# Two weight pairs of the input projection ahead of the first norm's product on TensorE

## The reference

```python
xn = rms_norm(h, g_mix[l])                 # x * rsqrt(mean(x^2) + eps) * g
proj = xn @ w_in[l]                        # 1024 -> 2564 columns
pa, pb, pc, pd = jnp.split(proj, ...)      # short conv, dilated attention, forgetting attention + 4 gates, pool
...
logf = jax.nn.log_sigmoid(p[..., 3 * G:] + b_f)      # the 4 gate columns
...
h = act(feat @ w1 + b1)                    # second block: hyena filter network, act(a) = sin(freq * a)
h = act(h @ w2 + b2)
h = act(h @ w3 + b3)
```

## Time and profile before

| | |
|---|---|
| Median of 3 runs | 1575.12 us (1574.12 to 1576.87) |
| Span of the profiled execution, first to last instruction | 1572.3 us |
| Median of the runs less that span | 2.8 us |
| TensorE busy | 1495.1 us, 95% |
| VectorE busy | 952.0 us, 61% |
| ScalarE busy | 572.7 us, 36% |
| GpSimd busy | 125.7 us, 8% |
| Mean granted TensorE clock | 0.972 of full speed |

### The profile page before, as it was taken

How to read it: one execution, slowest core, us unless ns; L and a number is a source line. 1 busy time by engine, 2 the same in 40 slices (tenths; PEclk the granted TensorE clock), 3 DMA queues, 4 the chain that set the end, 5 groups by cost and what they waited for, 6 DMA issues and landing times.

```text
span 1572.3 us, 17974 instructions
## 1 busy us (share of the span) xinstructions
PE 1495.1 (95%) x6732; PEld 1210.7 (77%) x6732; DVE 952.0 (61%) x1215; ACT 572.7 (36%) x740; POOL 125.7 (8%) x117
## 2 busy tenths in 40 slices
PE   6999999879998999999999999999899999999996
PEld 5678667657886888888888778887688888888884
DVE  6776665763554567547637787789766533443346
ACT  4321562441433354323314454543333321321222
POOL 1000131220000000000000110154100000000000
PEclk8899999889999999999999999999999999999998
DMA  5222115114320222223232232234232323222231
GB/s 208 89 75 90 65 54 188 41 54 187 107 81 28 81 80 107 82 106 107 81 108 87 100 108 107 80 126 139 83 107 86 112 97 107 80 107 99 89 107 53
DMA packets 23486, 153.08 MB, mean 97 GB/s; under 512 B 2811, under 2 KB 2955, under 8 KB 7040
## 3 DMA queue, kind: packets, MB, share of 16 engines
q1 hardware_dynamic: 18720, 134.23, 24.1%
q0 software_dynamic: 3984, 15.68, 2.9%
q10 hardware_dynamic: 720, 2.30, 0.4%
HBM read 145.90 MB, written 6.30 MB: 97 GB/s over the span
## 4 chain that ended last, share of the span: by engine, by line
PE 86%; DVE 8%; ACT 3%; issue 2%; DMA 1%; POOL 0%; SPq 0%; DVEq 0%; ACTq 0%; POOLq 0%
PE ps L1359 26%; PE ps L1361 26%; PE ps L1360 26%; DVE w_lo L724 1%; PE ps L1698 1%; DMA raw<-weights_dram 1%; DVE opA_lo L767 1%; PE ps L1539 1%; ACT w_hi L392 1%; PE ps L1590 1%; PE ps L1558 1%; PE ps L1460 1%; PE ps L1685 1%; PE ps L1548 1%; DVE gen L1027 1%
## 5 line engine op out<-in xcount | busy, mean ns | idle before, releaser
L1359 PE MATMUL ps<-opA_hi,w_hi 128*128 128x512 f32 x1184 | 470.4, 397 | 15.3 <-DVE opA_lo L775 11.7
L1361 PE MATMUL ps<-opA_hi,w_lo 128*128 128x512 f32 x1184 | 464.5, 392 | 0.0
L1360 PE MATMUL ps<-opA_lo,w_hi 128*128 128x512 f32 x1184 | 464.5, 392 | 0.0
L392 ACT CAST w_hi<-raw 128x2048 fp32r<-128x2048 f32 x119 | 227.2, 1909 | 386.9 <-PE ps L1361 382.7
L724 DVE TENSOR_TENSOR w_lo<-raw,w_hi 128x2048 fp32r<-128x2048 f32 x119 | 277.8, 2335 | 126.0 <-ACT w_hi L392 125.8
L1359 PEld LDWEIGHTS ps<-opA_hi,w_hi 128*128 128x128 f32 x1184 | 224.8, 190 | 68.3 <-DVE w_lo L724 12.7
L1360 PEld LDWEIGHTS ps<-opA_lo,w_hi 128*128 128x128 f32 x1184 | 224.9, 190 | 47.4 <-issue 1.4
L1361 PEld LDWEIGHTS ps<-opA_hi,w_lo 128*128 128x128 f32 x1184 | 224.4, 190 | 47.8
L1359 PE MATMUL ps<-opB_hi,w_hi 128*128 128x512 f32 x608 | 238.9, 393 | 7.3 <-DVE spec L1251 2.6
L1360 PE MATMUL ps<-opB_lo,w_hi 128*128 128x512 f32 x608 | 238.1, 392 | 0.0
L1361 PE MATMUL ps<-opB_hi,w_lo 128*128 128x512 f32 x608 | 237.9, 391 | 0.0
(11 more groups left out here) (276 smaller groups left out, 1585.0 us busy)
## 6 DMA issues: line engine op xcount, KB each, us to landing
raw<-weights_dram SPq DMA_DIRECT2D x126, 1024.0 KB, 4.8
g_dram<-gen POOLq DMA_DIRECT2D x8, 512.0 KB, 3.6
h<-x_t_dram SPq DMA_DIRECT2D x4, 512.0 KB, 11.1
h<-x_t_dram POOLq DMA_DIRECT2D x1, 2048.0 KB, 12.4
scores<-g_dram POOLq DMA_DIRECT2D x4, 512.0 KB, 3.6
g_spec<-g_dram POOLq DMA_DIRECT2D x4, 512.0 KB, 3.6
out_dram<-h ACTq DMA_DIRECT2D x4, 512.0 KB, 2.7
mem_raw<-mem_t_dram POOLq DMA_DIRECT2D x1, 1024.0 KB, 10.7
```

The source lines that it names most:

```text
L392: A.copy(w_hi[:, p, :], raw[:, p, :]).then_inc(hi_ready, 1)
L1359: W.matmul(out, w[0], x[0], start=start, stop=False)
L1360: W.matmul(out, w[0], x[1], start=False, stop=False)
L1361: return W.matmul(out, w[1], x[0], start=False, stop=stop)
```

## The change

TensorE's calls of `in_pair(1, 0)` and `in_pair(1, 1)` move from behind `mlp(0)` to directly behind `in_pair(0, 1)`, ahead of the norm's product. No instruction is added or taken away, no other engine's stream is touched, and no semaphore count is changed.

```diff
@@ -1447,8 +1447,10 @@
-            in_pair(0, 0)
-            in_pair(0, 1)
+            for j in range(2):
+                in_pair(0, j)
+            for j in range(2):
+                in_pair(1, j)
             pe.wait_ge(made_ones, 1)
             pe.wait_ge(summed, KT)
             W.matmul(misc(0), ones[:], acc[:], start=True, stop=True).then_inc(misc_done, 1)
@@ -1463,8 +1465,6 @@
             last.then_inc(misc_done, 1)
             pe.wait_ge(small_in, 112)
             mlp(0)
-            for j in range(2):
-                in_pair(1, j)
```

## The result

| | median (range, runs) | span of the profiled execution |
|---|---|---|
| before | 1574.62 us (1573.32 to 1576.87, 4 runs) | 1572.3 us |
| changed | 1580.28 us (1579.3 to 1583.72, 4 runs) | 1577.5 us |

The ratio is 1.0041 with a 95% interval of 1.0027 to 1.0055. The forecast was 1580.9 us within 1577.4 to 1583.9, slower. The change costs 5.7 us by the medians and 5.2 us by the spans.

The account below looks back on a forecast made before the run. TensorE, busy 95% of the span, was taken as the bound. Own time -4.7, stall at rotate(0, 4) +8.2, slower second rotation +0.2 and restart +2.0 gave +5.8 us (rounded): 1580.9 us, range 1577.4 to 1583.9.

Parts of the forecast that it names:

- Step 1: Behind chunk 1: chunks 2 and 3 run gapless at full clock to 35.94, saving TensorE 4.7 us of gap and restart.
- Step 2: At the norm's product: it starts at 35.94 instead of 27.67, delaying VectorE and ScalarE by 8.3 us.
- Step 3: From norm to mlp(0) reads: faster gates help little; VectorE and ScalarE stay 8.3 us late, second read ending at 62.95.
- Step 4: At rotate(0, 4): TensorE waits for VectorE's reads, some 8 us in two pieces, products at 58.7 and 62.95.
- Two terms of the sum: TensorE's own time, -4.7 us, and its standing still at rotate(0, 4), +8.2 us.
- Step 5: After the stall: second rotation at half clock, chunks 4 and 5 take 12.95 us, ending at 77.86, +5.8 us.
- The term of 2.0 us: Chunks 4 and 5: the cost of restarting at half clock, 12.95 us instead of 10.94.
- Step 6: Behind chunk 5: VectorE is ready at 76.1, ahead of 77.86, so TensorE sets the pace and nothing is given back.
- Moves rigidly from there: Everything behind chunk 5 (cast of pair 4, rope(2, 6), mlp(1), chunk 6) comes 5.8 us later.
- TensorE's own time decides: Rival: saved gap and restart count, VectorE's reads come in time; -4.7 us, 1570.4 us, chance 0.04.
- The clock stays full at rotate(0, 4): Rival: no half-clock restart after the stall; +2.7 us, 1577.8 us, chance 0.07.
- A second slow spell: Rival: another stretch of the head also starts at half clock; +7.8 us, 1582.9 us, chance 0.08.

Follow-up runs that it names:

- e12: Changed kernel with rotate(0, 4) behind chunks 4 and 5 and VectorE's two mlp(0) reads back to back: ratio 1.0018, chunk 6 2.0 us late.
- e8: The changed kernel run and profiled once more, unaltered, against the kernel before: ratio 1.0041, median 1584.11 against 1576.54 us.
- e11: Kernel before, with VectorE's rotary arguments put ahead of its read of the norm's product: ratio 0.9998.
- e10: Only chunk 2 (24 matmuls) ahead of the norm's product, VectorE's rotary arguments ahead of its norm read: ratio 0.9981 to the kernel before, median 1572.65 us.
- e4: Chunks 2 and 3 placed between the norm's product and the gates, so the norm stays on time: ratio 1.0045 to the kernel before.
- e6: Changed kernel with VectorE's two reads of mlp(0) back to back, ahead of both reductions: ratio 1.0006 to the kernel before.
- e7: Kernel before, with VectorE's two reads of mlp(0) back to back, ahead of both reductions: ratio 1.0001.
- e1: Only 12 of pair 1's 48 matmuls ahead of the norm's product, the other 36 behind mlp(0): ratio 0.9988 to the kernel before.

## Why the prediction was right

**Step 1** held: 48 matmuls without a gap, the norm's product at 35.80 in the chain of waits, against 35.94.

**Step 2** held but for 0.4 us: VectorE reads the norm 7.9 us later (36.70 against 28.81), not 8.3. Part of it is that the product behind dense work takes 0.87 us in the chain where it took 1.10 after the gap.

**Step 3** held in what it says of VectorE and ScalarE: line 814 ends at 50.34, the cast of pair 2 starts at 52.42 (52.8 was forecast), though the gates gained more than the one or two blocks. Three blocks of 16 started at full clock, and the clock fell only in the window from 41 to 42 us (0.96). It helped nothing, since VectorE came to the gates at 50.25, 3.3 us after they had ended (46.92), and read them without waiting.

**Step 4** held within 0.4 us: the two halves at 58.35 and 62.59 (58.7 and 62.95 forecast), idle 5.79 + 2.16 = 7.95 us ("some 8"). Two terms of the sum were off by 2 us and cancel. By the faster gates TensorE came to `rotate(0, 4)` at 52.56 (58.35 - 5.79), 6.9 us earlier than before and not 4.7, and then took 10.0 us to the second half, not 8.2. That they cancel is no accident: the second half goes when VectorE has read, whenever TensorE comes.

**Step 5** was right in kind and too dear. Chunks 4 and 5 took from 64.66 to 76.19, 11.53 us, not 12.95, because only three matmuls ran at half clock. In the second profile they took from 65.28 to 77.84, 12.56 us. The term of 2.0 us measured 0.6 in the one and 1.6 in the other. The forecast 77.86 for the end of chunk 5 was met by the second execution, which was 0.6 us late before the stall already, and missed by 1.7 us in the first. (One of the step's rows is miscounted: from 81.13 to 84.41 there are 7 slow matmuls, and the eighth, of 0.29, follows. Its bound of +5.5 comes out all the same.)

**Step 6** held for the first half: VectorE was still ahead of chunk 5, but with 0.67 us to spare in place of 1.8. That margin matters more than the prediction made of it: by e12 (2.0) VectorE would have held the loss in the head at about 2 us, had TensorE's stall been smaller.

"Moves rigidly from there" held roughly. Chunk 6 starts 4.1 us late, line 1529 at 169.2 is 4.7 us late (164.5 before), and the end 5.2: the distance doesn't shrink again. From the start of chunk 6 to the end of the span, the kernel before took 1491.2 us and the changed one 1492.3. That the total of 5.2 and 5.7 lies so near to the forecast 5.8 is in part luck: the head of that execution cost 1.7 us less than forecast, and 1.1 came back behind it for reasons that the prediction doesn't name. e8, with 6.5 to 7.6 us for the same kernel, lies on the other side.

Over the twelve profiles of the experiments the part behind the head took 1490.5 (e11) to 1496.0 us (e10), and it doesn't go with the head: the shortest head (e10) and the longest (e8, 1495.8) both stand at the top. In most runs of e8 the time was higher than its head explains: two runs gave 1579.7 and 1579.9 us at a mean granted clock of 0.971 and 0.970, the other six 1583.7 to 1585.0 at 0.967 to 0.968. So the clock in later stretches goes with it, and the ratios differ from the head's delay by up to 4 us (e4: head 2.9, time 7.1; e6: head 2.9, time 0.9). One such stretch can be seen in windows of 10 us, columns as in the earlier trace rows. First the kernel before, then e7:

```profile
1100.00:1110.00 10.00, 7.27 (x32) 5.72 (x31) 5.26 (x2) 1.90 (x1) 0.90 (x1) 1.00 0.62 239
```

```profile
1100.00:1110.00 10.00, 7.25 (x25) 5.54 (x24) 5.91 (x2) 1.90 (x1) 1.55 (x2) 0.83 0.64 236
```

TensorE is idle for about as long in both, but the granted clock is 1.00 in one and 0.83 in the other, and the distance between the two grows by 1.6 us from 1103 to 1119 us, by the starts of VectorE's low parts there. e7, with a head as long as that of the kernel before, ends 2.3 us later, so such a stretch comes without a longer head too. Whether the layout of the head makes a slow later stretch more likely in e4 and e8 is not settled; it would take many profiles of one kernel, and each run here has one.

**The rivals.** "TensorE's own time decides" would have needed the second read by about 54 us: with it there (e1, 54.54) the same idea does gain, with 62.54 it doesn't. The Trainium skill's advice on contiguous work (TensorE: Matmul & The Clock Gate, section "HAM oscillation — how this bites in real kernels") agrees with the 12 matmuls that fit the gap. For 48 it closed a gap of 2.7 us and opened two of 7.95. "The clock stays full at rotate(0, 4)" didn't happen in either profile of the changed kernel: 0.50 in the window from 62 to 63 us of the first, and in both the second rotation takes 2.08 us. "A second slow spell" wasn't needed for the result, though e8, at 7.6 us by the medians, came near its 7.8.

```profile
41.00:42.00 1.00, 1.00 (x11) 1.00 (x10) 0.93 (x3) 0.00 (x0) 0.00 (x0) 0.96 0.00 0
62.00:63.00 1.00, 0.41 (x1) 0.41 (x2) 0.95 (x2) 0.47 (x1) 0.00 (x0) 0.50 0.00 0
...
65.00:66.00 1.00, 1.00 (x4) 0.78 (x3) 0.96 (x3) 0.00 (x0) 0.00 (x0) 0.60 0.00 0
66.00:67.00 1.00, 1.00 (x6) 0.82 (x5) 1.00 (x3) 0.92 (x2) 0.00 (x0) 1.00 0.00 0
```

These are windows of 1 us of the changed kernel, columns as in the earlier trace rows: the clock falls during the gates and is back at the end of the first tile of chunk 4.

## What to carry to other kernels

Dense work that stands behind a small product often covers another engine's chain; before moving it ahead, follow that chain to the point where the busy engine needs its result, and compare its length with what is left over it. Fill a gap with as much work as fits into it (12 matmuls here: 2.7 us of gap filled and faster gates behind them, 4.2 us gained in the head) and not with all that is ready. When the waiting engine has work of its own that doesn't need the late result, put it into the wait first: alone it was worth nothing (e11), together with a chunk moved ahead it made the fastest kernel (e10).

## What the runs showed of the hardware that was not expected

The same program came back to full clock at different points: after three slow matmuls of chunk 4 in one execution and after eight in another, with the same waits ahead of them. The gates varied in the same way: their third block of 16 took 2.22 us in the first profile of the changed kernel and 3.33 us in e8. And full clock nearly halves the time of even matmuls of 4 columns: a block of 16 with its two products of one column takes 2.01 us at full clock (38.42 to 40.43) and 3.84 at half (31.20 to 35.04 in the kernel before), so the time of these small products, each with a weight load of 128 columns, goes with TensorE's clock.
